# Samples' index scores started inside the second pass of the projections, without a barrier; admission of three prompt tiles set into the prompt attention

## The chip, the cores and the metric

The kernel runs on one core of a Trainium2 chip. The metric is the device time of one execution in microseconds (us), lower is better. The engines are named PE (matrix multiply; PEld is its weight load), DVE (vector), ACT (scalar, activations), POOL (GpSimd) and SP (which here only starts transfers).

## The reference

One step of a hybrid decoder layer over 1024 prompt tokens and 64 sample tokens (8 samples of 8 tokens, each with 2048 past tokens in a paged cache):

```python
u, q, k, v, qi, ki, wi = project(rms_norm(h), w_in)      # one projection, 1864 columns
q, k, qi, ki = rope(...)                                  # partial rotary
pool_o = pool_mix(u_ext, ...)                             # windows 2/4/8/16, then a 128x128 map per group
# indexer: 8 heads, one shared key per token
s = einsum('bthd,bsd->bths', qi, ki) * IDX_DIM ** -0.5
score = einsum('bths,bth->bts', relu(s), wi)              # causal
_, sel = top_k(score, 256)                                # each query keeps 256 keys
attn_o = sparse_attend(q, k[sel], v[sel])                 # prompt: own keys; samples: paged cache and own keys
h = h + concat(pool_o, attn_o) @ w_out
h = h + hier_moe(rms_norm(h), ...)                        # top-2 of 8 experts in 1 of 4 groups
```

## The kernel before

Tokens are cut in nine tiles: eight of 128 prompt tokens and one of the 64 sample tokens, which is worked on first (`ORDER`). The engines run hand-written instruction streams that meet at semaphores, and at four barriers on which all engines wait. PSUM has eight banks; each stage gives them names (`PART` for stage 1, `P2A` for 2a), an order of uses written out by hand (`order`, `orderA`), and a pair of semaphores per bank: PE "claims" a bank (waits until the use before was emptied), another engine "takes" it when it is filled. `SAME` says which bank of stage 2a carries on the counts of which bank of stage 1.

- **Stage 1, first pass.** Keys, values, index queries of each tile; for prompt tiles 2 to 7 the index scores (PE L1079, relu on ACT L1592, weighted sum on DVE L1966). The steps of tile n's scores are a generator, `scores(n)`, of which other loops pull a piece after each of their matmuls.
- **Stage 1, second pass.** For each of nine rounds n: `pool_inputs(n)` (PE L1107), `q_turn(n-1)` (transposes of rotated queries, L1127), `queries(n)` (L1118), `pool_out(n-1)` (L1139), `u_turn(n-1)` (L1150). The last prompt tile's scores are pulled from `pool_inputs(0)`; round 3 begins with the transposes of the pooling state (L1171). POOL computes the windows (`pooling(n)`) and rotates the queries (`rope_q(n)`, L821 to L824). ACT empties the banks (L1533) and between them runs 18 coarse bisection rounds for the prompt tiles 2, 3, 4 ("near"; L1657, L1661, L1665).
- **Beside it, on DVE:** the bisection of each row's threshold. `halve` counts the scores above a middle value (L2002, one pass over the row) and makes three short steps; 26 rounds for the prompt tiles 5, 6, 7 ("far"), then `admit` for each (five long operations, L2026 to L2040, which write the mask), then 10 fine rounds and `admit` for the near tiles, then `masks_ready`.
- **Barrier `phase1`** (PE, ACT, DVE, POOL; SP's loads of `w_out` and the router wait on it too).
- **Stage 2a**, the samples' index scores: for each sample b POOL gathers its 2048 paged index keys (`index_keys(b)`, L895, 512 KB) into one of two buffers, PE turns them (`ki_turn`, L1197), ACT copies them, PE multiplies (`s_scores`, L1208), ACT takes the relu (L1734), and PE sums the heads into three banks with a weight matrix `WD` (`weighted`, L1221) that POOL builds after the barrier (L923, L928). At the end ACT copies the sums into `SCs`, in order of tokens (five copies).
- **Barrier `phase2a`.**
- **Stage 2b**, attention of the prompt tiles: 32 steps (tile i, head pair h). "S": PE multiplies queries and keys (L1249), DVE adds the mask and takes the maximum (L2337), ACT takes the exponential (L1780). "T": PE turns the probabilities (L1260), ACT copies. "V": times the values (L1272). Among them are the output projection (OP, L1302; DVE adds the residual, L2287) and the router's logits. The bisection over the samples' rows (64 x 2056) is done meanwhile on DVE, as a generator `selections()`: after a step of kind S or V of tile i, DVE pulls `PIECES[i][kind]` pieces. Its pieces are: one that does nothing, two reductions (L1977, L1979), 26 rounds of four pieces of which one is a pass (L2002), and the admission.
- **Stage 2c** is the samples' attention, then follow the experts and the last norm.

A second use of memory matters: the two key buffers are `rl` and the last 1024 words; the region behind `w_out`'s place overlays the normalised input `xnT`.

Of the kernel before, what the change touches and what calls it, by code (L numbers as in the profile page):

```python
# [22 lines left out]
P = 128  # L23
# [34 lines left out]
PIECES = [{"S": 2}] + [{"S": 4}] * (NT - 2) + [{"S": 1, "V": 1}]  # L58
# [67 lines left out]
def program(nc, x_prompt, x_sample, cache_k, cache_v, cache_idx_k, state_pool, page_table, norm_mix_g, w_in,  # L126
# [5 lines left out]
    with ctx:  # L132
# [58 lines left out]
        Z = cut(2 * 12 * HD, (2, 12, HD))  # L191
        Zq = cut(2 * NH * HD, (2, NH, HD))
        rt1 = cut(11 * ROPE, (11, ROPE))
        rt2 = cut(11 * ROPE, (11, ROPE))
        rounds = cut(3 * COARSE, (3, COARSE))
# [5 lines left out]
        kin = [v.rearrange("p (s d) -> p s d", s=SLOTS) for v in (rl[:, :, :].rearrange("p a b -> p (a b)"), mem[:, TOTAL - 1024:TOTAL])]  # L201
# [28 lines left out]
        region = at[0]  # L230
        kiTs = cut(2 * 1024, (2, 8, P))
        rs = cut(2 * HLS, (2, HLS))
        zslots = cut(NBLK * 16, None, I32)
        WD = cut(SB * (P + ST))
        assert at[0] <= TOTAL
# [307 lines left out]
        SAME = {"2aACC": "1B4", "2aTR0": "1T0", "2aTR1": "1T1", "2aPS0": "1S0", "2aPS1": "1S1", "2aPS2": "1B5"}  # L543
# [49 lines left out]
        ki_in = [sem(f"ki_in{s}") for s in range(2)]  # L593
# [12 lines left out]
        masks_ready = sem("prompt_masks_ready")  # L606
# [190 lines left out]
        def _(pool):  # L797
# [93 lines left out]
            def index_keys(b):  # L891

                if b >= 2:
                    take(pool, "2a", "TR1", b - 2)
                pool.indirect_dma_start(kin[b % 2].rearrange("p s d -> p (s d)"), None, ci_rows,  # L895
                                        bass.IndirectOffsetOnAxis(ap=pidx[:, b:b + 1], axis=0)).then_inc(ki_in[b % 2], 16)
# [7 lines left out]
            for n in range(TILES):  # L904
                pooling(n)
                rope_q(n)
                if n == 3:
# [7 lines left out]
            copied(pool, "1", "T0", ("q", 0))  # L915
            for g in range(NKV):
                q0 = qT[HD * g:HD * (g + 1), :, SEQ:NTOK].rearrange("p h (b t) -> p b h t", b=SB)
                link(pool.tensor_copy(QB[HD * g:HD * (g + 1), :, g, :, :], q0))
# [3 lines left out]
            pool.wait_ge(phase1, 4)  # L922
# [8 lines left out]
            for b in range(2, SB):  # L931
                index_keys(b)

# [6 lines left out]
            for s in range(2):  # L940
                pool.wait_ge(ki_in[s], 16 * SB // 2)
# [81 lines left out]
        def _(pe):  # L1023
# [73 lines left out]
            def pool_inputs(n, between):  # L1097
# [13 lines left out]
            def queries(n):  # L1111
# [7 lines left out]
                ins.then_inc(filled["1B4"], 1)  # L1119
# [36 lines left out]
            for n in range(TILES):  # L1156
# [5 lines left out]
                for _ in between:  # L1162
                    pass
            between = scores(TILES - 1)
            next(between)
            for n in range(TILES + 1):
                if n == 3:
                    pe.wait_ge(state_in, 16)
                    claim(pe, "1", "T0", "state")
                    for g in range(4):  # L1170
                        ins = tr(ps[:, 0, g * SB * HALO:(g + 1) * SB * HALO], stt_in[0:SB * HALO, g * P:(g + 1) * P], ident(SB * HALO))  # L1171
                    ins.then_inc(filled["1T0"], 1)
                if n < TILES:
                    pool_inputs(n, between)
                    for _ in between:
                        pass
                if n:
                    q_turn(n - 1)
                if n < TILES:
                    queries(n)  # L1180
# [4 lines left out]
            settle(pe, "1")  # L1185
            pe.drain().then_inc(phase1, 1)
            pe.wait_ge(phase1, 4)

            def ki_turn(b):
                pe.wait_ge(ki_in[b % 2], 16 * (b // 2 + 1))
                for c in range(2):
                    claim(pe, "2a", f"TR{c}", b)
                    for j in range(4):
                        a = 2 * (4 * c + j)
                        ins = tr(ps[:, 3 + c, j * P:(j + 1) * P], kin[b % 2][:, a:a + 2, :].rearrange("p s d -> p (s d)"), ident(P))  # L1197
# [31 lines left out]
            for b in range(SB):  # L1229
# [3 lines left out]
                if b:  # L1233
                    weighted(b - 1)
# [294 lines left out]
        def _(act):  # L1529
# [164 lines left out]
            for n in range(TILES + 1):  # L1694
                if n == 3:
                    take(act, "1", "T0", "state")
                    copy(uS[:, :, :, 0:HALO], ps[:, 0, 0:4 * SB * HALO].rearrange("p (g b t) -> p g b t", g=4, b=SB))\
                        .then_inc(emptied["1T0"], 1)
                if n < TILES:
                    keep_u(n)  # L1700
                    some_rounds(n)
# [3 lines left out]
                if n < TILES:  # L1705
                    keep_queries(n)
# [818 lines left out]
```

## Time and profile before

| | us |
|---|---|
| three runs | 1226.13, 1226.91, 1229.39 (median 1226.91) |
| the profiled execution | 1225.94, of which the span of the trace is 1224.10 |
| stage 1 until the barrier | 0 to 334.2 |
| stage 2a until the barrier | 334.2 to 386.6 |
| stage 2b, from the first mask on DVE to the first of tile 7 | 387.65 to 590.96 |
| granted TensorE clock, mean | 0.944 |

In the rows further down a group of instructions stands with its start and its time on the chip; a source line in brackets or behind an arrow is what ended the idle time before it. Windows give the busy time of each engine within a stretch.

### The profile page before, as it was taken

Reading aid. Unit: us, or ns where it says so; the run is one execution under the profiler, and the core shown is the slowest. Engines: PE = TensorE matmul, PEld = TensorE weight load, DVE = VectorE, ACT = ScalarE, POOL = GpSimd, SP = SyncE. Lnnn points to the kernel's source line nnn. Section 1 sums busy time; section 2 is a strip of 40 time slices with the busy share of each in tenths; the row PEclk is TensorE's granted clock in tenths of the full one; section 3 lists DMA queues with packets and bytes.
Section 4 is the critical chain, followed back from the end, with each engine's and each line's share of the span. In section 5 each row is a group of like instructions: output and inputs, shape, how many; then the busy total and the mean of one; then the engine's idle time right before and its main releaser. Section 6 shows DMA issues by size and latency. Waiting matters only on the chain.

```text
span 1224.1 us, 16550 instructions
## 1 busy us (share of the span) xinstructions
PE 1085.3 (89%) x6208; PEld 732.9 (60%) x6208; DVE 581.1 (47%) x1282; ACT 413.1 (34%) x976; POOL 205.7 (17%) x256
## 2 busy tenths in 40 slices
PE   4999989899886999999997898499999999999920
PEld 2554433354343677777775556287878778788720
DVE  2234568999997777666462361213111111111138
ACT  1234445567534345555541333211111110111113
POOL 1432215354421000000012200000000000000032
PEclk9999999999988699999999899699999999999965
DMA  6510000010095911110012741499899999998757
GB/s 215 197 46 12 12 22 1 1 35 5 9 239 198 278 53 52 52 53 35 36 35 78 301 181 70 146 371 372 303 345 339 334 350 329 331 352 326 271 181 281
DMA packets 71372, 209.54 MB, mean 171 GB/s; under 512 B 11214, under 2 KB 31774, under 8 KB 61061
## 3 DMA queue, kind: packets, MB, share of 16 engines
q1 hardware_dynamic: 57119, 151.75, 35.1%
q0 software_dynamic: 10448, 44.21, 10.7%
q10 hardware_dynamic: 3742, 12.75, 2.7%
q8 instruction: 38, 0.62, 0.2%
q14 instruction: 25, 0.20, 0.1%
HBM read 171.40 MB, written 37.40 MB: 171 GB/s over the span
## 4 chain that ended last, share of the span: by engine, by line
PE 80%; DVE 9%; ACT 3%; DMA 3%; issue 2%; POOL 1%; SPq 0%; POOLq 0%; ACTq 0%; DVEq 0%; PEldq 0%
PE ps L1457 18%; PE ps L1463 10%; PE ps L1302 8%; PE ps L1091 5%; PE ps L1107 5%; PE ps L1118 5%; PE ps L1046 3%; PE ps L1079 3%; PE ps L1249 3%; PE ps L1260 2%; PE ps L1450 2%; PE ps L1272 2%; ACT mem L1533 2%; DVE mem L2002 2%; PE ps L1313 1%
## 5 line engine op out<-in xcount | busy, mean ns | idle before, releaser
L1533 ACT ACTIVATE mem<-ps 128x512 f32<-128x512 f32 (+10 forms) x376 | 172.6, 497 | 330.7 <-PE ps L1463 64.1
L1457 PEld LDWEIGHTS ps<-mem 128*128 128x128 f32 x2048 | 235.4, 193 | 16.8 <-issue 16.8
L1457 PE MATMUL ps<-mem 128*128 128x96 f32 x2048 | 234.9, 276 | 0.8 <-DVE mem L2404 0.8
L2002 DVE TENSOR_SCALAR_CACHE_REDUCE mem<-mem 128x768 bf16<-128x768 f32 (+2 forms) x134 | 166.5, 1283 | 0.0
L1302 PE MATMUL ps<-mem 128*128 128x256 f32 (+1 forms) x544 | 126.6, 385 | 5.8 <-ACT mem L1533 2.8
L1463 PE MATMUL ps<-mem 128*96 128x512 f32 x256 | 119.3, 609 | 2.4 <-DVE mem L2396 2.3
L1302 PEld LDWEIGHTS ps<-mem 128*128 128x128 f32 (+1 forms) x544 | 100.1, 189 | 23.1 <-ACT mem L1533 3.7
L2396 DVE TENSOR_TENSOR mem<-mem,ps 128x192 f32<-128x192 f32 x32 | 11.4, 356 | 212.7 <-ACT mem L1873 212.7
L1873 ACT ACTIVATE mem<-ps 128x192 f32<-128x192 f32 x32 | 10.6, 333 | 264.0 <-PE ps L1457 264.0
L983 POOL DMA_INDIRECT mem<-xn_rows,mem x32 | 29.0, 905 | 369.4 <-PE ps L1450 317.6
L1463 PEld LDWEIGHTS ps<-mem 128*96 128x96 f32 x256 | 39.6, 164 | 58.5 <-issue 52.4
L1091 PE MATMUL ps<-mem 128*128 128x512 f32 (+1 forms) x144 | 70.9, 610 | 0.0
L2337 DVE CUSTOM_DVE_ANT_0 mem<-ps,mem 128x128 f32<-128x128 f32 (+7 forms) x64 | 48.2, 754 | 47.0 <-PE ps L1249 47.0
L2411 DVE COPY mem<-ps 96x512 f32<-96x512 f32 x32 | 22.1, 689 | 102.0 <-PE ps L1463 102.0
L1107 PE MATMUL ps<-mem 128*128 128x512 f32 (+1 forms) x192 | 68.1, 505 | 0.0
L1118 PE MATMUL ps<-mem 128*128 128x512 f32 (+1 forms) x144 | 63.4, 593 | 0.0
L1966 DVE SCALAR_TENSOR_TENSOR mem<-mem 128x512 f32<-128x512 f32 (+3 forms) x70 | 47.0, 672 | 19.1 <-ACT mem L1592 14.6
L1260 PE MATMUL ps<-mem 128*128 128x128 f32 x288 | 46.7, 290 | 7.1 <-ACT mem L1780 5.5
L1592 ACT ACTIVATE mem<-ps 128x512 f32<-128x512 f32 (+3 forms) x80 | 38.5, 523 | 38.0 <-PE ps L1079 33.0
L1780 ACT ACTIVATE mem<-mem 128x128 f32<-128x128 f32 (+7 forms) x64 | 49.3, 773 | 5.2 <-DVE mem L2340 5.0
L1107 PEld LDWEIGHTS ps<-mem 128*128 128x128 f32 x192 | 31.3, 194 | 32.9 <-issue 32.9
L1260 PEld LDWEIGHTS ps<-mem 128*128 128x128 f32 x288 | 32.5, 145 | 25.8 <-issue 18.1
(292 smaller groups left out, 1387.2 us busy)
## 6 DMA issues: line engine op xcount, KB each, us to landing
mem<-in_expert_w_gate SPq DMA_DIRECT2D x32, 1024.0 KB, 5.5
mem<-in_expert_w_up SPq DMA_DIRECT2D x32, 1024.0 KB, 8.7
mem<-in_expert_w_down SPq DMA_DIRECT2D x32, 1024.0 KB, 10.9
expert_rows<-mem ACTq DMA_DIRECT2D x32, 384.0 KB, 8.0
expert_rows<-mem SPq DMA_DIRECT2D x2, 4608.0 KB, 30.3
mem<-in_x_prompt SPq DMA_DIRECT2D x16, 512.0 KB, 4.3
mem<-in_w_in SPq DMA_DIRECT2D x3, 2048.0 KB, 10.8
h_rows<-mem SPq DMA_DIRECT2D x8, 512.0 KB, 2.6
```

The source lines that it names most:

```text
L1091: ins = mm(ps[0:r, 4, :], xnT[:, k, tok], w1[:, k, NKI:NIN - CK], start=(k == 0), stop=(k == KC - 1))
L1107: ins = mm(out, w2[:, k, g * P:(g + 1) * P], xnT[:, k, tok], start=(k == 0), stop=(k == KC - 1))
L1118: ins = mm(ps[0:r, 4, :], xnT[:, k, tok], w2[:, k, CQ:CK], start=(k == 0), stop=(k == KC - 1))
L1260: ins = tr(ps[:, 4 + part, (j - c) * P:(j - c + 1) * P], Sm[:, u % 2, g, j * P:(j + 1) * P], ident(P))
L1302: ins = mm(ps[0:r, 7, 0:256], lhs, wout[:, k, 256 * t[2]:256 * t[2] + 256], start=(k == 0), stop=(k == last))
L1457: ins = mm(ps[:, 2 + s, j * CAP:(j + 1) * CAP], wgu[w][:, j // 2, k, (j % 2) * P:(j % 2 + 1) * P], xgT[:, s, k, :], start=(k == 0), stop=( ...
L1463: ins = mm(ps[0:CAP, 5 + c, :], hT[:, s, k, :], wdn[w][:, k, 512 * c:512 * (c + 1)], start=(k == 0), stop=(k == 1))
L1533: return fn(out, in_, ACT.Copy, scale=scale)
L1780: fn(probs, probs, ACT.Exp, bias=nb[:, c:c + 1], scale=SCALE, accum_out=esum[:, 8 * (i % 2) + c:8 * (i % 2) + c + 1]).then_inc(s_exp, 1)
L1966: v.scalar_tensor_tensor(out=dst, in0=src, scalar=wt, in1=dst, op0=ALU.mult, op1=ALU.add).then_inc(score_added, 1)
L2002: v.tensor_scalar(bufs[a % 3][0:R, 0:w], sc, mid[:, a:a + 1], None, ALU.is_ge, ALU.add, accum_out=cnt[:, a:a + 1]).then_inc(step, 1)
L2337: v.tensor_tensor_reduce(out=Sm[:, u % 2, g, 0:w], in0=sc2, in1=maskv(i), scale=1.0, scalar=-3e38, op0=ALU.add, op1=ALU.max, accum_out=mx[ ...
```

## The change

Seven edits, all in the order of work and in the place of buffers; the arithmetic is the same.

1. Four key buffers in place of two. Buffers 2 and 3, the turned keys `kiTs` and the relus `rs` lie over `xnT`, `WD` over the rotated queries `Zq`. POOL issues the gathers 2 and 3 right behind its last `rope_q`, waits for all four, and builds `WD` as soon as the last queries were turned, before the barrier.
2. PE goes from round 8 of the second pass straight on to stage 2a: `ki_turn(0)`, `s_scores(0)`, `ki_turn(1)`, then the last queries, pooling and state turns, then samples 1 to 7. The barrier `phase1` is signalled by PE after `ki_turn(2)`, by ACT after `keep_ki(3)`; neither waits on it. SP and POOL still do.
3. The bank names of 2a are laid on other counts of stage 1.
4. In the second pass the last prompt tile's scores are pulled from the fourth matmul of `pool_inputs(0)` on and from `queries(0)`; before, their first step (the transposes of `z_turn(8)`) stood ahead of `pool_inputs(0)`.
5. The turn of the pooling state moves from the start of round 3 to behind `queries(3)`.
6. The last copy of 2a is shared: ACT copies the even slots, DVE the odd ones; ACT runs a small exponential ahead of it.
7. DVE's admission of the near tiles moves behind the barrier `phase2a`, into the generator of stage 2b, ahead of the samples' selection (18 pieces and the first of `select`, the nineteenth). `PIECES` grows from 112 to 136 in all. The first gathers of stage 2c, which wait on `masks_ready`, move with it; the clearing of the overflow rows no longer waits on it.

```diff
-PIECES = [{"S": 2}] + [{"S": 4}] * (NT - 2) + [{"S": 1, "V": 1}]
+PIECES = [{"S": 2, "V": 1}, {"S": 1, "V": 1}] + [{"S": 5, "V": 1}] * 2 + [{"S": 4, "V": 1}] * 3 + [{"S": 1, "V": 1}]
...
-            if n == 3:
-                order += [("T0", "state")]
...
+                if n == 3:
+                    order += [("T0", "state")]
...
-        SAME = {"2aACC": "1B4", "2aTR0": "1T0", "2aTR1": "1T1", "2aPS0": "1S0", "2aPS1": "1S1", "2aPS2": "1B5"}
+        SAME = {"2aACC": "1T0", "2aTR0": "1S3", "2aTR1": "1B4", "2aPS0": "1B5", "2aPS1": "1S0", "2aPS2": "1S1"}
...
-                if b >= 2:
-                    take(pool, "2a", "TR1", b - 2)
+                if b >= 4:
+                    take(pool, "2a", "TR1", b - 4)
...
-            for s in range(2):
+            for b in (2, 3):
+                index_keys(b)
+            for s in range(4):
                 pool.wait_ge(ki_in[s], 16)
...
             pool.wait_ge(kv_out, 48 * TILES)
             pool.drain().then_inc(phase1, 1)
-            pool.wait_ge(phase1, 4)
+            take(pool, "1", "T0", ("q", TILES - 1))
             link(pool.memset(WD[:, :], 0.0))
...
-            for b in range(2, SB):
+            for b in range(4, SB):
                 index_keys(b)
+            pool.wait_ge(phase1, 4)
...
+            pool.wait_ge(phase2a, 3)
+            pool.memset(zrow, 0.0).then_inc(zrow_ready, 1)
             pool.wait_ge(masks_ready, 1)
             past(Kin, ck_rows, 0, K_in)
             past(Kin, ck_rows, 1, K_in)
-            pool.wait_ge(phase2a, 3)
             past(Vin, cv_rows, 0, V_in)
-            pool.memset(zrow, 0.0).then_inc(zrow_ready, 1)
...
-                        next(between, None)
+                        if k >= 3:
+                            next(between, None)
...
             between = scores(TILES - 1)
-            next(between)
-            for n in range(TILES + 1):
...
+            for n in range(TILES):
+                pool_inputs(n, between)
                 if n:
                     q_turn(n - 1)
-                if n < TILES:
-                    queries(n)
+                queries(n, between)
+                for _ in between:
+                    pass
+                if n == 3:
+                    state_turn()
                 if n:
                     pool_out(n - 1)
...
-            settle(pe, "1")
-            pe.drain().then_inc(phase1, 1)
-            pe.wait_ge(phase1, 4)
...
             ki_turn(0)
-            for b in range(SB):
+            s_scores(0)
+            ki_turn(1)
+            q_turn(TILES - 1)
+            pool_out(TILES - 1)
+            u_turn(TILES - 1)
+            for b in range(1, SB):
                 s_scores(b)
                 if b + 1 < SB:
                     ki_turn(b + 1)
-                if b:
-                    weighted(b - 1)
+                if b == 1:
+                    settle(pe, "1")
+                    pe.drain().then_inc(phase1, 1)
+                weighted(b - 1)
...
+            fn(stat[:, 254:255], const("z"), ACT.Exp)
             take(act, "2a", "ACC", 0)
...
-            for a in range(2):
-                for q in range(2):
-                    copy(inorder[:, 8 * q + a:8 * q + a + 7:2, :], ps[a * SR:(a + 1) * SR, q, :].rearrange("r (s p) -> r s p", s=4))
+            for q in range(2):
+                copy(inorder[:, 8 * q:8 * q + 7:2, :], ps[0:SR, q, :].rearrange("r (s p) -> r s p", s=4))
...
+            act.wait_ge(odd_slots_kept, 1)
...
             halvings(near, 0, FINE)
-            admit_group(near, 0)
-            dve.nop().then_inc(masks_ready, 1)
+            take(dve, "2a", "ACC", 0)
+            inorder = SCs[0:SR, 0:PAST].rearrange("r (p s) -> r s p", s=SLOTS)
+            for q in range(2):
+                ins = v.tensor_copy(inorder[:, 8 * q + 1:8 * q + 8:2, :], ps[SR:2 * SR, q, :].rearrange("r (s p) -> r s p", s=4))
+            ins.then_inc(odd_slots_kept, 1)
...
             def selections():
+                unhalve(near, 0)
+                for a, entry in enumerate(near):
+                    yield from admit(entry, a)
+                dve.nop().then_inc(masks_ready, 1)
+                near_admitted.append(True)
                 yield from select([(SCs[0:SR, :], LS, SR, const("tailmask", SR), None, (sJ, sG, sT))], 6, sample_step, admitted)
```

## Rows read from the trace of the kernel before

**Rows 1.** The page's busy times and share of the span, instructions.

```profile
PE 1085.3 (89%) x6208; PEld 732.9 (60%) x6208; DVE 581.1 (47%) x1282; ACT 413.1 (34%) x976; POOL 205.7 (17%) x256
```

**Rows 2.** Stretch, length, busy PE, PEld, DVE, ACT, POOL, granted clock, DMA share, GB/s.

```profile
192.94:336.65 143.71, 133.60 (x396) 64.25 (x395) 139.20 (x298) 85.69 (x268) 71.23 (x92) 0.97 0.04 11
336.65:365.20 28.55, 22.77 (x88) 13.56 (x87) 27.03 (x103) 10.77 (x24) 4.92 (x6) 0.84 0.97 255
365.20:380.00 14.80, 14.80 (x58) 8.31 (x57) 13.83 (x26) 6.75 (x15) 2.71 (x5) 1.00 0.18 60
380.00:387.65 7.65, 3.30 (x13) 1.71 (x12) 0.38 (x5) 3.92 (x5) 2.70 (x3) 0.93 0.74 265
```

**Rows 3.** PE in order of time where the second pass begins.

```profile
171.29 0.99 PE L1061 MATMUL ps<-mem 128*128 128x128 f32 x4 [3.30 <-POOL mem L836]
174.34 1.38 PE L1079 MATMUL ps<-mem 64*128 64x512 f32 x4
190.45 7.08 PE L1118 MATMUL ps<-mem 128*64 128x512 f32 x16
```

**Rows 4.** The chain of waits around round 3 and at the end of the second pass.

```profile
227.10 0.02 issue
...
232.87 8.57 PE ps L1107 x16
...
317.90 6.88 PE ps L1118 x16
```

**Rows 5.** POOL in order of time: first queries rotated, last ones, `WD`.

```profile
201.67 0.45 POOL L824 TENSOR_TENSOR mem<-mem 64x128 f32<-64x128 f32 x1
...
280.41 0.32 POOL L822 TENSOR_TENSOR mem<-mem 128x64 f32<-128x64 f32 x1
...
326.12 1.05 POOL L822 TENSOR_TENSOR mem<-mem 128x64 f32<-128x64 f32 x1
...
334.25 1.01 POOL L923 MEMSET mem<- 128x1088 f32 x1 [4.58 <-ACTq L1718]
335.34 1.43 POOL L928 TENSOR_TENSOR mem<-mem 64x64 f32<-64x64 f32 x2
```

**Rows 6.** The gathers of index keys: all eight, then the two of round 3.

```profile
DMA to landing us min/median/max: 4.1/6.7/10.9
...
mem<-in_cache_idx_k,mem POOLq DMA_INDIRECT x2, 4.4
```

**Rows 7.** PE in stage 2a: the wait for keys, the sums at either clock.

```profile
348.08 1.97 PE L1197 MATMUL ps<-mem 128*128 128x128 f32 x8 [5.53 <-DMA mem<-in_cache_idx_k,mem]
349.84 3.27 PE L1221 MATMUL ps<-mem 128*128 128x512 f32 x6
355.81 2.01 PE L1221 MATMUL ps<-mem 128*128 128x512 f32 x6
```

**Rows 8.** Copies at 2a's end on ACT, table load, DVE's nearest copies from PSUM.

```profile
382.63 3.94 ACT L1533 ACTIVATE mem<-ps 64x512 f32<-64x512 f32 x5 [3.43 <-PEq L1226]
388.22 1.28 ACT L1780 ACT_TABLE_LOAD   x1 [1.65 <-DVE mem L2340]
...
411.49 0.68 DVE L2277 TENSOR_TENSOR mem<-ps,mem 128x512 f32<-128x512 f32 x1
```

**Rows 9.** Busy time in tiles 0, 1, 2, 3 and 4 to 6 of stage 2b.

```profile
387.65:403.01 15.36, 8.65 (x36) 4.46 (x36) 13.10 (x38) 6.53 (x24) 0.39 (x2) 0.50 1.02 323
403.01:425.67 22.66, 21.07 (x96) 13.88 (x96) 17.19 (x55) 7.79 (x25) 0.00 (x0) 0.69 1.01 294
425.67:451.86 26.19, 25.82 (x160) 18.87 (x161) 20.47 (x57) 14.28 (x32) 0.00 (x0) 1.00 0.18 64
451.86:482.56 30.70, 30.18 (x204) 22.79 (x205) 21.74 (x59) 16.06 (x32) 0.00 (x0) 1.00 0.15 52
482.56:590.96 108.40, 106.20 (x790) 82.40 (x791) 71.69 (x174) 59.95 (x119) 0.00 (x0) 1.00 0.12 45
```

**Rows 10.** One pass of the samples' bisection on DVE.

```profile
427.63 2.34 DVE L2002 TENSOR_SCALAR_CACHE_REDUCE mem<-mem 64x2056 bf16<-64x2056 f32 x1
```

More of the change, by code:

```diff
@@ L592, in program @@
         pidx_ready = sem("page_rows_ready")
-        ki_in = [sem(f"ki_in{s}") for s in range(2)]
+        ki_in = [sem(f"ki_in{s}") for s in range(4)]
         sample_step = sem("sample_step")
@@ L906, in _ @@
                 rope_q(n)
+                if n == 2:
+                    copied(pool, "1", "T0", ("q", 0))
+                    for g in range(NKV):
+                        q0 = qT[HD * g:HD * (g + 1), :, SEQ:NTOK].rearrange("p h (b t) -> p b h t", b=SB)
+                        link(pool.tensor_copy(QB[HD * g:HD * (g + 1), :, g, :, :], q0))
                 if n == 3:
@@ L939, in _ @@
             pool.wait_ge(slots_cleared, 16)
-            for s in range(2):
-                pool.wait_ge(ki_in[s], 16 * SB // 2)
+            for s in range(4):
+                pool.wait_ge(ki_in[s], 16 * SB // 4)
             pool.drain().then_inc(phase2a, 1)
@@ L1118, in queries @@
                     ins = mm(ps[0:r, 4, :], xnT[:, k, tok], w2[:, k, CQ:CK], start=(k == 0), stop=(k == KC - 1))
-                ins.then_inc(filled["1B4"], 1)
+                    if k == KC - 1:
+                        ins.then_inc(filled["1B4"], 1)
+                    next(between, None)
             def q_turn(n):
@@ L1163, in _, with state_turn @@
                     pass
-            between = scores(TILES - 1)
-            next(between)
-            for n in range(TILES + 1):
[L1167 to L1172, printed above, removed]
-                if n < TILES:
-                    pool_inputs(n, between)
-                    for _ in between:
-                        pass
+            def state_turn():
+                pe.wait_ge(state_in, 16)
+                claim(pe, "1", "T0", "state")
+                for g in range(4):
+                    ins = tr(ps[:, 0, g * SB * HALO:(g + 1) * SB * HALO], stt_in[0:SB * HALO, g * P:(g + 1) * P], ident(SB * HALO))
+                ins.then_inc(filled["1T0"], 1)
+            between = scores(TILES - 1)
+            for n in range(TILES):
+                pool_inputs(n, between)
                 if n:
                     q_turn(n - 1)
-                if n < TILES:
-                    queries(n)
+                queries(n, between)
[3 more added lines that the diff above has]
+                    state_turn()
                 if n:
@@ L1692, in some_rounds, with keep_state, keep_ki, relus_of @@
                     next(between, None)
[L1694 to L1701, printed above, removed]
+            def keep_state():
+                take(act, "1", "T0", "state")
+                copy(uS[:, :, :, 0:HALO], ps[:, 0, 0:4 * SB * HALO].rearrange("p (g b t) -> p g b t", g=4, b=SB))\
+                    .then_inc(emptied["1T0"], 1)
+            def keep_ki(b):
+                for c in range(2):
+                    take(act, "2a", f"TR{c}", b)
+                    copy(kiTs[:, b % 2, 4 * c:4 * c + 4, :], four(ps[:, 3 + c, :], P)).then_inc(emptied[f"2aTR{c}"], 1)
+            def relus_of(b):
+                for q in range(3):
+                    w = 512 if q < 2 else ST
+                    take(act, "2a", f"PS{q}", b)
+                    if b >= 2 and q == 0:
+                        act.wait_ge(sec_done, b - 1)
+                    fn(rs[:, b % 2, 512 * q:512 * q + w], ps[:, 5 + q, 0:w], ACT.Relu).then_inc(emptied[f"2aPS{q}"], 1)
+            for n in range(TILES):
+                keep_u(n)
+                some_rounds(n)
                 if n:
@@ L1704, in _ @@
                     some_rounds(n)
[L1705 to L1707 removed]
+                keep_queries(n)
+                if n == 3:
+                    keep_state()
+                some_rounds(n)
                 if n:
@@ L1714, in _ @@
                 pass
+            keep_ki(0)
+            relus_of(0)
+            keep_ki(1)
+            keep_q(TILES - 1)
+            keep_pool(TILES - 1)
+            keep_u_turned(TILES - 1)
             copied(act, "1", "T0", ("u", TILES - 1))
             act.dma_start(pool_prompt[0, 0], ut[0:HALO, :]).then_inc(u_out, 16)
[L1717 to L1734 removed]
+            for b in range(1, SB):
+                relus_of(b)
                 if b + 1 < SB:
                     keep_ki(b + 1)
+                if b == 2:
+                    act.wait_ge(u_out, 16 * (SB + 1))
+                    act.drain().then_inc(phase1, 1)
+            fn(stat[:, 254:255], const("z"), ACT.Exp)
             take(act, "2a", "ACC", 0)
             inorder = SCs[0:SR, 0:PAST].rearrange("r (p s) -> r s p", s=SLOTS)
[L1739 to L1742 removed]
+            for q in range(2):
+                copy(inorder[:, 8 * q:8 * q + 7:2, :], ps[0:SR, q, :].rearrange("r (s p) -> r s p", s=4))
+            copy(SCs[0:SR, PAST:LS], ps[0:SR, 2, 0:ST])
+            act.wait_ge(odd_slots_kept, 1)
+            act.nop().then_inc(emptied["2aACC"], 1)
             act.drain().then_inc(phase2a, 1)
```

45 lines of the change are left out of this document (16 added, 29 removed).

## The prediction

> **What bounds the kernel now.** The page comes first: PE is busy 89% of the span, DVE 47% [rows 1]. As averages these point at PE and hide the stretch that matters. The view by stretches shows it: from 192.94 to 336.65 DVE is busy 139.20 of 143.71 us (bounds, 26 rounds, admission of the far tiles), to 365.20 it is busy 27.03 of 28.55 us (the fine rounds of the near tiles), to 380.00 it is busy 13.83 of 14.80 us (their admission); then it stands for 7 us [rows 2]. PE in the same stretches is busy too, but with a second pass and stage 2a whose end nobody but stage 2b needs. So two chains run side by side to the start of 2b: DVE's, without holes until 380.00, and PE's, with holes. PE's comes last, at 386.6 [rows 8]. Whatever shortens PE's chain gains only down to DVE's, and DVE's needs its own cut; the change makes both.
>
> The PE views in order of time give PE's holes: 3.30 us for the rotation of the last keys at 171.29, with a slow start behind it [rows 3]; 227.10 to 232.87 at round 3, with 0.6 us of work of its own, and 8.57 us for the sixteen matmuls behind it where 6.9 is the rule [rows 4]; from 324.8 to 334.25 the tail of the second pass and the barrier [rows 4, 5]; 5.53 us for the third gather [rows 7].
>
> **PE's chain after the change.**
> - Start of the second pass. Three matmul pairs of `pool_inputs(0)` (3 x 0.86 = 2.6 us; sixteen matmuls take 6.88 [rows 4]) now fill the 3.30 us. Without the slow start the first scores come about 1.3 us before 174.34, and so do all DVE times from 192.94 on. PE has four of the eight k-steps of `queries(0)` behind it when the scores end (3.5 us). Together 4.8 us. But the next queries turn needs POOL's rotation, which ended at 202.1 [rows 5] and starts only 1.3 us earlier: PE is held about 1.2 us. Gain 3.6.
> - Round 3. The hole is there because the state turn's bank waits for ACT's copy behind five bisection pieces. Behind `queries(3)` that copy is long done. 5.77 - 0.6 = 5.2 less, and 1.7 for the slow matmuls behind it; `pool_out(1)` and the turn behind it, some 1.1 us, lie in the hole and stay. Gain 5.8. So the second pass ends at 324.8 - 9.4 = 315.4.
> - Stage 2a. POOL's last rotation ends 4.0 us later (324.8 to 328.85 before), 319.4. Gathers 2 and 3 are issued by 321.6 and land by 326 at 4.4 us each [rows 6]. `WD` costs 1.01 + 1.43 plus gaps, 2.7 us, behind their landing: 328.8. PE meanwhile does `ki_turn(0)` to `s_scores(1)`, `ki_turn(2)` and the last turns (316.3 to 326.2), then stands 2.6 us for `WD`. Before, from the start of the first sums at 349.84 to the end at 382.5 it was 32.7 us, at a cold first group (3.27 where 2.01 is the rule [rows 7]): 31.4 warm. PE's sums are ready at 328.8 + 31.4 = 360.2. Gathers 4 to 6 are issued by 332, ahead of SP's loads, which wait for the barrier (ACT behind `keep_ki(3)`, about 334); gather 7 has over 10 us.
> - SP's loads of `w_out` thus start when they did before (334.2) and are first needed in tile 1 of 2b: no cost. SP's queue holds nothing else. The clearing of 9.2 MB starts some 20 us sooner and ahead of the K gathers; nobody waits for either until 2c.
>
> **DVE's chain after the change.** 365.20 - 1.3 = 363.9, later than PE's 360.2, so DVE decides. Its two copies of 64 x 512 from PSUM aren't in the trace. Below: 0.68 each, its own 128 x 512 operation; above: 0.95, ACT's strided ones (3.94 for four and a small one) [rows 8]. I take 0.8, since the store is strided: 365.5; two more semaphores, 365.8 for the first matmul of 2b against 386.67. ACT's half ends by 362.2 and is hidden. **Start of 2b: -20.9 us** (bounds -21.5 and -18: if the gathers land in 10.9 us like the one in the worst row [rows 6], `WD` comes at 335 and PE's chain ends at 367; ACT and DVE add 2).
>
> **Stage 2b.** Now the 14.80 us of admission must be done before the masks of tile 2. Count the pieces: tiles 0 and 1 pulled 24 of the samples' selection, now 19, of which 18 are admission. In DVE's time: 24 pieces are two reductions of 2.3 and 5.2 rounds of 2.9 (a pass of 2.34 [rows 10] and four short steps), some 20 us; 19 are 14.8. From step to step:
> - Tile 0 took 15.36 us with DVE 13.10 busy and PE at half clock [rows 9]. The table load of 1.28 us [rows 8] is done ahead; the pieces of the small tiles are short. I get steps of 2.4, 3.2, 2.6 and 3.7: 11.9. Tile 1 is bound by PE at half clock (21.07 busy of 22.66): about 21.4. Gain 4.7.
> - Tiles 2 and 3 pull 24 pieces each, not 16: two rounds, 5.8 us more per tile. Tile 2 has 26.19 - 20.47 = 5.7 us of DVE idle, tile 3 has 9.0 [rows 9]: the sum fits, but not evenly. Five pieces at S hold one pass or two, and S(2,0) gets both reductions and a pass (6.9 us). DVE's residual adds queue behind them, and PE's next claim of bank 7 behind those. Against the old gaps between masks S(2,0) is 4.5 late, S(2,1) 1.8, S(3,1) 2.1: 8.4 if nothing hides it, 3.3 if PE's work between its scores and its turns (about 3 us) hides its part. I take 5.5.
> - Tiles 4 to 6 pull one piece more at each V, a whole pass in one V per tile. DVE is idle 36.7 of 108.4 us there. I take 1 us, bounds 0 and 3.
> - Tile 7 has fewer pieces left than before: 0.
>
> Net for 2b: -4.7 + 5.5 + 1 = **+1.8**, bounds -5 and +7. Stages 2c, experts and last norm are as before; the K gathers land some 290 us before 2c.
>
> [...] POOL's step L822 took 0.32 us while DVE counted and 1.05 while it admitted tiles with two inputs from SBUF [rows 5]. [...]
>
> The table load is 1.28 us in its row [rows 8]; "ScalarE: Activation LUTs", section "What ACT_TABLE_LOAD costs", of the Trainium skill gives 2.66 with its drain. By the one tile 0 gains 1.3, by the other 2.7; no row here shows the drain.
>
> **The sum.** Against the profiled execution of 1225.94: -20.9 + 1.8 = -19.1, 1206.8. The three runs' median stands 1.0 higher. I say **1207**.
>
> **The rivals.**
> - *A, as above: DVE's fine rounds set the start of 2b, 2b about even.* 1202 to 1213. Chance 0.66.
> - *B, 2b becomes DVE's.* All 14.8 us of the admission come back as time, since DVE was busy 13.10 of 15.36 in tile 0 and 20.47 of 26.19 in tile 2. Against: PE was busy 21.07 of 22.66 in tile 1, and five pieces less are pulled ahead of tile 2. 1225.9 - 20.9 + 14.8 = 1220. Chance 0.12.
> - *C, PE's chain decides after all:* slow gathers, the port, `WD` late, a half clock behind the 2.6 us wait. 1225.9 - 18 + 1.8 = 1210, and with a stall at each of gathers 4 to 6 (5.5 each) up to 1218. For: 10.9 us in one row. Against: PE has 3.7 us of slack, and four gathers are landed or under way. Chance 0.07.
> - *D, the double passes are hidden.* In before PE hardly waits for DVE in tiles 2 and 3 (25.82 of 26.19, 30.18 of 30.70 busy). 1225.9 - 20.9 - 4.7 = 1200, less if tile 1 leaves half clock sooner. Chance 0.12.
> - *E, slower.* Every step of tiles 2 and 3 exposes a whole round: PE claims bank 7 for the next projection, the claim waits for the residual add, and that stands behind the five pieces. 8 x 2.9 = 23.2, so 1228 to 1231. It decides only from 20.9 / 2.9 = 7.2 exposed rounds on; the two tiles get four rounds more in all, and their DVE idle of 14.7 us speaks against it. Chance 0.03.
>
> **Range and chances.** 1207 from A. The range 1199 to 1215 takes in A, D and most of C, leaving out B and E. About 0.3% of the time, 4 us, is what a measurement can tell from nothing. Faster by more: A, B (6 us), C, D: 0.94; within: 0.03, a B or C gone worse; slower: 0.03.
>
> **What would show it.** Right: DVE goes from its last fine round into the two copies with hardly a wait, about 364, and PE's sums are ready some 4 us before; first mask of 2b near 366.8; the turn of the state without a wait; PE's second pass ending near 315.4; tile 2's first mask near 400, tile 4's near 463. Wrong: DVE waiting for the sums at its copies (C); masks of tiles 2 and 3 each late with no idle time on DVE (B, E); tile 1 at full clock from its start (D, and lower).

## The result: 1217.9 us, and the profile after

The changed kernel takes 1217.9 us (median of 4 runs, 1216.23 to 1218.22); the kernel before, beside it, 1227.09 (4 runs, 1226.13 to 1229.39). The ratio is 0.992, interval 0.9903 to 0.9937: faster by 9 us, where 20 were forecast. The profiled execution took 1218.01 us, its span is 1216.2, against 1225.94 and 1224.10: 7.9 us less. The working below is made on these two.

The page says nothing of this, as before [rows 1]: nearly the same instructions and busy shares.

```profile
PE 1079.9 (89%) x6208; PEld 732.2 (60%) x6208; DVE 580.9 (48%) x1284; ACT 411.7 (34%) x975; POOL 205.8 (17%) x256
```

The view by stretches of the kernel after, with the columns of [rows 2]: the first three lines reach to the first mask of stage 2b, then come tiles 0, 1, 2, 3 and 4 to 6, each from its first mask to the next tile's.

```profile
190.90:333.85 142.95, 134.37 (x420) 66.56 (x419) 138.21 (x300) 91.09 (x282) 74.28 (x95) 0.99 0.05 16
333.85:362.40 28.55, 28.55 (x113) 16.37 (x112) 27.04 (x103) 12.63 (x28) 4.95 (x7) 0.96 0.93 238
362.40:368.85 6.45, 3.91 (x16) 1.94 (x14) 2.25 (x8) 3.48 (x7) 0.21 (x1) 1.00 0.24 86
368.85:380.25 11.40, 8.43 (x36) 4.22 (x36) 10.37 (x41) 5.72 (x24) 0.00 (x0) 0.57 1.01 309
380.25:400.77 20.52, 19.34 (x95) 13.02 (x96) 12.20 (x40) 7.28 (x24) 0.77 (x1) 0.74 1.00 291
400.77:437.24 36.47, 28.60 (x160) 20.17 (x161) 30.41 (x74) 14.57 (x32) 2.12 (x3) 0.93 0.44 160
437.24:474.27 37.03, 32.25 (x204) 24.53 (x205) 27.20 (x70) 15.99 (x32) 0.00 (x0) 0.93 0.12 43
474.27:583.98 109.71, 106.46 (x791) 82.54 (x792) 79.15 (x193) 60.57 (x119) 0.00 (x0) 1.00 0.12 44
```

Set against [rows 9], this is the ledger: the first mask comes at 368.85 instead of 387.65 (-18.8); tiles 0 and 1 take 31.9 instead of 38.0 (-6.1); tiles 2 and 3 take 73.5 instead of 56.9 (**+16.6**); tiles 4 to 6 take 109.7 instead of 108.4 (+1.3). Sum -7.0, and 0.9 comes behind it. So 25 us were won ahead of tile 2 and 17 given back in two tiles. In those two the granted clock fell to 0.93, from 1.00 before.

The chain of waits of the kernel after (start, length, what), at round 3, at the end of the second pass, and from there to the first sums of stage 2a:

```profile
200.90 0.46 POOL mem L830
201.41 0.46 PE ps L1140 x4
...
239.11 0.41 PE ps L1181 x4
...
308.69 6.88 PE ps L1129 x16
...
320.72 5.18 DMA mem<-in_cache_idx_k,mem
326.10 2.60 POOLq L929
328.69 0.11 issue
328.80 1.02 POOL mem L932
329.89 0.99 POOL mem L937
330.95 1.32 POOL mem L937
332.32 4.01 PE ps L1229 x6
```

PE is held for POOL's rotation at 200.90, as forecast; the turn of the state (L1181) follows its neighbours without a hole; the second pass ends at 315.58 (forecast 315.4). Then a term appears that the forecast hadn't: 2.60 us on POOL's queue at L929, its drain for the barrier, which stands ahead of `WD`. The chain of waits of the kernel before had such a row too, for the same drain (L920 there), ahead of the barrier:

```profile
329.71 2.44 POOLq L920
```

What follows `WD` in the kernel after, in the views in order of time of PE, ACT and DVE:

```profile
332.32 4.01 PE L1229 MATMUL ps<-mem 128*128 128x512 f32 x6 [6.97 <-POOL mem L937]
...
362.53 1.28 ACT L1759 ACT_TABLE_LOAD   x1
...
365.94 1.88 ACT L1548 ACTIVATE mem<-ps 64x512 f32<-64x512 f32 x3 [1.92 <-PEq L1234]
```

```profile
366.01 1.87 DVE L2161 COPY mem<-ps 64x512 f32<-64x512 f32 x2 [3.62 <-PEq L1234]
```

DVE was done with its fine rounds at 362.4 and waited 3.62 us for the sums. The forecast had it the other way round: sums ready at 360.2, DVE at 363.9. The sums were ready at 365.8, 5.6 us later than said: 3.5 because they began at 332.32 and not at 328.8, and 2.1 because they took 33.5 us for 31.4. The forecast had taken full clock, but behind PE's wait of 6.97 us the first group took 4.01 us for 2.01, and the granted clock from 332.30 to 339.10 is 0.70; from 339.10 on it is 1.00. The copies cost 1.87 (1.6 said), and the table load lies in the wait.

### Where tiles 2 and 3 lose their time

First the kernel before, DVE in the first step of tile 2. Behind the pass at 427.63 [rows 10] comes the residual add (L2287), and then DVE waits for PE's next scores:

```profile
429.90 0.41 DVE L2287 TENSOR_TENSOR mem<-ps,mem 128x256 f32<-128x256 f32 x1
...
431.40 0.56 DVE L2337 CUSTOM_DVE_ANT_0 mem<-ps,mem 128x384 f32<-128x384 f32 x1 [0.52 <-PE ps L1249]
```

Of the 14.7 us that DVE is idle in tiles 2 and 3, 11.4 are such waits, one in each of the eight steps.

DVE in order of time at the start of tile 2 (kernel after):

```profile
402.10 2.28 DVE L2001 TENSOR_REDUCE mem<-mem 64x1 f32<-64x2056 f32 x1
404.30 2.28 DVE L2003 TENSOR_REDUCE mem<-mem 64x1 f32<-64x2056 f32 x1
...
407.30 2.33 DVE L2026 TENSOR_SCALAR_CACHE_REDUCE mem<-mem 64x2056 bf16<-64x2056 f32 x1
...
409.94 0.43 DVE L2314 TENSOR_TENSOR mem<-ps,mem 128x256 f32<-128x256 f32 x1
```

and PE in the same place:

```profile
400.92 3.62 PE L1317 MATMUL ps<-mem 128*128 128x256 f32 x16
410.43 5.41 PE L1317 MATMUL ps<-mem 128*128 128x256 f32 x16 [3.49 <-DVE mem L2314]
...
418.06 0.66 PE L1301 MATMUL ps<-mem 128*128 128x128 f32 x4 [1.42 <-DVE mem L2314]
```

PE's waits between 400 and 475, summed by what they waited for (total, times, longest):

```profile
PE ps L1322 <- DVE mem L2314: 5.0, 2, 2.6
PE ps L1301 <- DVE mem L2314: 3.8, 2, 2.4
PE ps L1317 <- DVE mem L2314: 3.5, 1, 3.5
```

The projection of 400.92 was finished at 404.5, but its residual add (L2314) stands behind three long operations and runs at 409.94. PE's next projection waits for it, 3.49 us, and then takes 5.41 us for what takes 3.62 elsewhere: after the wait PE is at a lower granted clock (0.68 from 410.43 to 415.80, where it was 1.00 from 400.77 to 410.93; from 404.5 to 410.4 PE had been busy 2.4 of 5.9 us). In the kernel before, PE's waits for the residual add make 0.3 us between 387 and 484; here the three rows make 12.3. Step by step, first mask to first mask, before and after: (2,0) 5.7 and 10.2, (2,1) 6.6 and 9.0, (2,2) 6.1 and 6.2, (2,3) 7.8 and 11.1; (3,0) 8.5 and 9.0, (3,1) 7.2 and 9.6, (3,2) 6.7 and 6.7, (3,3) 8.3 and 11.7. The five long ones are (2,0), which has both reductions and a pass ahead of its add, and (2,1), (2,3), (3,1), (3,3), which have two passes ahead of it. DVE's idle time stayed as it was, 6.1 and 9.8 us in the two tiles for 5.7 and 9.0 before: none of the extra work went into it.

### The profile page after: what moved, and what is told of

It reads as the page before. It is cut to its first block, busy times and chain, and to the rows that moved or that the text cites. A ratio compares the mean times of both kernels' runs of the same rounds, so it can differ in the third digit from the quotient of the medians.

```text
span 1216.2 us, 16556 instructions
## 1 busy us (share of the span) xinstructions
PE 1079.9 (89%) x6208; PEld 732.2 (60%) x6208; DVE 580.9 (48%) x1284; ACT 411.7 (34%) x975; POOL 205.8 (17%) x256
## 4 chain that ended last, share of the span: by engine, by line
PE 76%; DVE 13%; DMA 3%; issue 2%; ACT 2%; POOL 2%; SPq 0%; POOLq 0%; ACTq 0%; DVEq 0%; PEldq 0%
PE ps L1472 18%; PE ps L1478 10%; PE ps L1317 6%; PE ps L1101 5%; PE ps L1129 5%; PE ps L1117 5%; DVE mem L2026 4%; PE ps L1056 4%; PE ps L1089 3%; PE ps L1264 2%; PE ps L1465 2%; PE ps L1275 2%; DVE mem L2372 2%; PE ps L1287 2%; PE ps L1328 1%
## 5 line engine op out<-in xcount | busy, mean ns | idle before, releaser
L1548 ACT ACTIVATE mem<-ps 128x512 f32<-128x512 f32 (+9 forms) x374 | 170.5, 495 | 317.0 <-PE ps L1275 62.9
L2431 DVE TENSOR_TENSOR mem<-mem,ps 128x192 f32<-128x192 f32 x32 | 11.4, 356 | 213.5 <-ACT mem L1897 213.5
L1101 PE MATMUL ps<-mem 128*128 128x512 f32 (+1 forms) x144 | 70.9, 610 | 0.0
L1117 PE MATMUL ps<-mem 128*128 128x512 f32 (+1 forms) x192 | 64.7, 489 | 0.0
L1129 PE MATMUL ps<-mem 128*128 128x512 f32 (+1 forms) x144 | 64.3, 595 | 0.0
L1990 DVE SCALAR_TENSOR_TENSOR mem<-mem 128x512 f32<-128x512 f32 (+3 forms) x70 | 47.0, 672 | 19.0 <-ACT mem L1607 14.4
L1275 PEld LDWEIGHTS ps<-mem 128*128 128x128 f32 x288 | 33.1, 147 | 23.0 <-issue 18.8
```

The costliest lines, as they stand in the source:

```text
L1101: ins = mm(ps[0:r, 4, :], xnT[:, k, tok], w1[:, k, NKI:NIN - CK], start=(k == 0), stop=(k == KC - 1))
L1129: ins = mm(ps[0:r, 4, :], xnT[:, k, tok], w2[:, k, CQ:CK], start=(k == 0), stop=(k == KC - 1))
L1275: ins = tr(ps[:, 4 + part, (j - c) * P:(j - c + 1) * P], Sm[:, u % 2, g, j * P:(j + 1) * P], ident(P))
L1548: return fn(out, in_, ACT.Copy, scale=scale)
```

## The experiments

Nine, in three batches. Each ratio is to the kernel before on the same chip.

**1. The same number of pieces, spread level.** Tiles 2 and 3 give one piece less per step, the last tile takes them.

```diff
-... + [{"S": 5, "V": 1}] * 2 + [{"S": 4, "V": 1}] * 3 + [{"S": 1, "V": 1}]
+... + [{"S": 4, "V": 1}] * 5 + [{"S": 2, "V": 1}]
```

> Theory L (lumps): in tiles 2 and 3 of stage 2b time is lost only in the steps whose five pieces hold two long operations ahead of the residual add that frees bank 7. With 4 pieces at every S of tiles 2 to 6, each S holds one pass; the four double steps (+2.4, +3.3, +2.5, +3.4 us in the changed kernel's trace) go back to the old length, S(2,0) stays long, and about two more passes at a V cost 0.5 to 0.8 each: 1218 - 10 = 1208. Theory T (load): DVE simply has too much to do in the two tiles; what counts is its total. Then only the eight pieces taken out (two rounds, 5.8 us) come off, and come back in part in later tiles: 1212 to 1215.

Measured 1222.58 (1218.74 to 1224.99, 9 runs), ratio 0.9968 (0.9952 to 0.9984): slower than the change, both expectations missed. Yet tiles 2 and 3 took 67.4 us in place of 73.5, and the last mask of 2b came at 606.96 in place of 613.78. The 6.8 us, and 2.4 more in the profiled executions, are lost behind it, where the samples' selection now ends too late. DVE and POOL at the end of 2b, in order of time:

```profile
609.62 4.42 DVE L2055 TENSOR_TENSOR_SCAN mem<-mem 64x2056 f32<-64x2056 bf16 x1
...
625.71 4.67 DVE L2384 COPY mem<-mem 128x512 f32<-128x512 f32 x1
```

```profile
620.75 9.34 POOL L968 TENSOR_SCALAR mem<-mem 64x2048 bf16<-64x2048 bf16 x1
```

The scan stands in the last steps, and the copy of 0.43 us lasts 4.67 and ends just behind POOL's operation of 9.34. By PE's waits the scan costs more than the copy: scan and pass stand ahead of a residual add (616.65), for which PE waits 3.96 us at 617.14, with a granted clock of 0.83 over the ten us behind it (1.00 in the same place of the changed kernel). The projection behind the copy waits 1.60 us in place of 0.29.

**2. The same pieces in the same steps, one of them behind the residual add.** This is the run that parts the theories: in tiles 2 and 3 four pieces at S, the fifth once the residual add is issued.

```diff
-... + [{"S": 5, "V": 1}] * 2 + [{"S": 4, "V": 1}] * 3 + [{"S": 1, "V": 1}]
+... + [{"S": 4, "V": 1}] * 5 + [{"S": 1, "V": 1}]
...
-                if i < NT:
+                if kind == "S":
+                    step_tile = i
+                if kind == "OP" and step_tile in (2, 3):
+                    some_pieces(1)
+                elif i < NT:
                     some_pieces(PIECES[i].get(kind, 0))
```

> The same number of pieces in each tile as in the changed kernel, but in tiles 2 and 3 the fifth piece of a step is pulled behind DVE's residual add, not ahead of it. Theory L: the double steps shorten, since PE's next claim of bank 7 no longer waits behind a second pass: 1218 - 8 to - 11 = 1207 to 1210. Theory T: DVE's load per tile is unchanged, so the time is too: 1217 to 1219.

Measured 1209.02 (1207.99 to 1210.28, 4 runs), ratio 0.9859 (0.9843 to 0.9874): 8 to 9 us better than the change (8.9 by the medians, 7.5 by the two ratios), with the pieces of every tile unaltered. Tiles 2 and 3 took 64.0 us in place of 73.5. So 9.5 of the 16.6 us are the order within a step, not the load. What is left against the 56.9 of before sits where a step holds more than one long operation: (2,0), with both reductions and a pass ahead of the add, stays at 10.05 against 5.73. A second pass behind the add costs 1.8 us in (2,1) and 0.8 in (3,1), and nothing in (2,3) and (3,3), which last 7.8 and 8.3 us as before the change.

**3. Only the admission put back** ahead of the last copies, where it stood before, with the pieces of before; all else as changed.

```diff
             halvings(near, 0, FINE)
+            admit_group(near, 0)
+            dve.nop().then_inc(masks_ready, 1)
...
             def selections():
-                unhalve(near, 0)
-                for a, entry in enumerate(near):
-                    yield from admit(entry, a)
-                dve.nop().then_inc(masks_ready, 1)
```

> Everything of the change but edit 7: the near tiles are admitted ahead of the last copy of 2a and PIECES is the old list. If DVE's chain then decides the start of 2b, its fine rounds end at 362.3, admission at 377, copies at 379, first mask at about 380.5 against 368.85; stage 2b is then as before less the table load. 1227 - 7 - 1.3 = about 1218.5, the same as the changed kernel: the move of the admission won 11.7 us ahead of 2b and lost it in tiles 2 and 3. If it were PE's chain that decides throughout, the time would be no later than the changed kernel's start of 2b with the old tiles: 1227 - 18.8 - 1.3 = 1207.

Measured 1216.54 (1215.67 to 1218.28, 4 runs), ratio 0.9926 (0.9911 to 0.9942). Here DVE is the later chain; windows of this kernel from the start of its fine rounds to their end and on to the first mask:

```profile
333.00:362.40 29.40, 29.40 (x117) 16.72 (x117) 27.95 (x106) 14.23 (x30) 4.59 (x6) 0.98 0.91 234
362.40:378.59 16.19, 2.38 (x10) 1.26 (x8) 14.72 (x28) 1.89 (x3) 0.83 (x2) 0.68 0.07 29
```

The first mask comes at 378.59, 9.7 us later than with the change. Up to the first mask of tile 2 the changed kernel is 14.4 us ahead of this one (400.77 and 415.12), since tiles 0 and 1 are shorter too. Tiles 2 and 3 take 56.9 us here and 73.5 there, 4 to 6 108.4 and 109.7. So edit 7 wins 9.7 us ahead of 2b and 4.6 in tiles 0 and 1 and, as it is placed, loses 17.9 in tiles 2 to 6. The ratios (0.9926 and 0.992) don't tell the two kernels apart.

**4. POOL's drain behind `WD`.** POOL still waits for all four gathers; its drain for the barrier moves from ahead of `WD` to behind it, and with it the wait for `kv_out`, which takes 0.04 us in the chain (326.01).

```diff
-            pool.wait_ge(kv_out, 48 * TILES)
-            pool.drain().then_inc(phase1, 1)
             take(pool, "1", "T0", ("q", TILES - 1))
             link(pool.memset(WD[:, :], 0.0))
...
                 pool.wait_ge(weights_spread, a + 1)
+            pool.wait_ge(kv_out, 48 * TILES)
+            pool.drain().then_inc(phase1, 1)
```

> POOL's drain ahead of the barrier (2.6 us in the trace) stands behind the building of WD, not ahead of it. If PE's chain decides the start of 2b in the changed kernel (sums ready at 365.8, DVE's fine rounds done at 362.3), the sums are ready 2.6 us earlier and the time falls by 2.5 us, to 1215.4. If DVE's chain decides, as the prediction had it, nothing changes.

Measured 1215.87 (1214.8 to 1218.34, 5 runs), ratio 0.9921 (0.9907 to 0.9935): 2.0 us under the change's median, but its ratio to the kernel before is that of the change (0.992), so the runs show no certain gain in time. The trace shows the mechanism: the sums begin 3.7 us sooner, and the first mask comes at 365.49, 3.4 us sooner, while DVE's fine rounds end where they did. PE's chain sets the start of 2b in the changed kernel. PE, then DVE, in order of time:

```profile
328.66 2.63 PE L1228 MATMUL ps<-mem 128*128 128x512 f32 x6 [3.33 <-POOL mem L934]
```

```profile
362.41 1.92 DVE L2160 COPY mem<-ps 64x512 f32<-64x512 f32 x2
```

DVE goes from its fine rounds into the copies without a wait, at 362.41. That is the state that the forecast had taken for the changed kernel's.

**5. Both, 2 and 4.**

> The two edits of x2_behind_add (fifth piece behind the residual add) and x4b_drain_behind (POOL's drain behind WD) together on the changed kernel. They act in different stretches, so they should add: 1217.9 - 8.9 - 2.0 = 1207. If the one only moves a wait into the other's stretch, it stays at 1209.

Measured 1207.44 (1206.02 to 1209.83, 5 runs), ratio 0.984 (0.982 to 0.9861). Against experiment 2 nothing certain is gained (1209.02 and 1207.44, the intervals of the ratios overlap); in its profiled execution the first mask came at 368.98. The last section tells why.

**6. The two reductions moved to tile 1**, so that no step of tile 2 has three long operations.

```diff
-PIECES = [{"S": 2, "V": 1}, {"S": 1, "V": 1}] + ...
+PIECES = [{"S": 2, "V": 1}, {"S": 2, "V": 1}] + ...
...
-                if kind == "OP" and step_tile in (2, 3):
+                if kind == "OP" and step_tile == 3:
```

> As y1_both, but tile 1 pulls two pieces at S (not one), and tile 2 none behind the residual add; the total of 136 stays. Both long reductions and the first pass then fall in tile 1, where DVE is busy 12.2 of 20.5 us, and S(2,0) holds one pass. Theory L: S(2,0) falls from 10.0 to about 6 and S(2,1) from 8.4 to 6.6, tile 1 grows by 0 to 2: 1207 - 4 to - 6 = 1201 to 1203. Theory T (load of DVE): the three long operations cost the same wherever they stand: 1206 to 1208.

Measured 1207.38 (1206.08 to 1211.67, 5 runs), ratio 0.9845 (0.9822 to 0.9869): a miss, nothing gained on experiment 5. Step (2,0) fell to 5.75 us, but (2,2) stands at 8.3 and (2,3) at 9.2, where a pass now falls on a V of tile 2, and tile 1 paid 2.9 us in its four steps (against 18.98 in experiment 5; against the 20.24 of experiment 2, with the same pieces in tile 1, it is 1.6). What a second pass behind the add costs hangs on the step: 2.2 us in (2,2) here, nothing in (3,3). Why is not shown.

**7. Level as in 1, but the selection finished sooner** by a second piece at V in tiles 5 and 6.

```diff
-... + [{"S": 4, "V": 1}] * 5 + [{"S": 2, "V": 1}]
+... + [{"S": 4, "V": 1}] * 3 + [{"S": 4, "V": 2}] * 2 + [{"S": 1, "V": 1}]
```

> x1_level won 6.8 us by tile 7's last mask against the changed kernel and lost more than that behind it: its samples' selection ended late, POOL's mask operation (9.3 us) fell on DVE's copy of the inverse sums, which took 4.67 us in place of 0.43, and its scan stood ahead of the last projections' adds. Here the same level pieces in tiles 2 and 3, but tiles 5 and 6 pull two pieces at V, so that the selection ends eight pieces sooner. If that collision is the cause: the copy is back at 0.43 and the time 1209 to 1213. If the level pieces themselves are bad: 1219 to 1222 as before.

Measured 1213.66 (1212.93 to 1214.13, 4 runs), ratio 0.9888 (0.9867 to 0.991). POOL's long operation now runs from 600.91, and the copy at 623.60 takes 0.43 us again. So the late selection was what cost experiment 1 its gain. The time is 0.7 us above the 1213 expected, and POOL's operation still holds DVE up: it now falls on DVE's multiplication of 1.29 us (L2323), which lasts 4.87 from 605.85, as it does in the changed kernel (4.38).

**8. The edits of the second pass undone** (4 and 5): the transposes ahead of `pool_inputs(0)`, the state turn at the start of round 3.

```diff
-                        if k >= 3:
-                            next(between, None)
+                        next(between, None)
...
-                    next(between, None)
...
             between = scores(TILES - 1)
+            next(between)
             for n in range(TILES):
+                if n == 3:
+                    state_turn()
                 pool_inputs(n, between)
+                for _ in between:
+                    pass
```

> The changed kernel with edits 4 and 5 undone: the state turn at the start of round 3 and the last prompt tile's scores pulled as before. PE's second pass should end 9.2 us later (324.8 for 315.6). PE's chain decides the start of 2b by 3.6 us already, so all of it comes through: 1227. Were DVE's chain the one that decides, only what goes beyond it: 9.2 less the slack that PE's chain has, 3 to 6 us, 1221 to 1224.

Measured 1228.01 (1227.5 to 1232.51, 10 runs), ratio 1.0009 (0.9997 to 1.0022): no gain over the kernel before. PE and DVE of this kernel in order of time:

```profile
341.92 4.01 PE L1228 MATMUL ps<-mem 128*128 128x512 f32 x6 [6.18 <-POOL mem L937]
```

```profile
376.06 1.94 DVE L2160 COPY mem<-ps 64x512 f32<-64x512 f32 x2 [9.64 <-PEq L1233]
```

The sums begin 9.6 us later than with the change (341.92 for 332.32), and DVE waits 9.64 us for them instead of 3.62; the first mask comes at 378.96, 10.1 later. The forecast of -9.4 for these two edits is borne out, and the median moves by the same ten.

**9. At most one pass ahead of a residual add, and none extra in tiles 2 and 3.** Experiment 5 with the extra pieces in tile 1 and in tiles 4 to 6, whose steps are longer; there they stand behind the residual add.

```diff
-PIECES = [{"S": 2, "V": 1}, {"S": 1, "V": 1}] + [{"S": 4, "V": 1}] * 5 + [{"S": 1, "V": 1}]
+PIECES = [{"S": 2, "V": 1}, {"S": 2, "V": 1}] + [{"S": 4}] * 2 + [{"S": 4, "V": 1}] * 3 + [{"S": 1, "V": 1}]
...
-                if kind == "OP" and step_tile in (2, 3):
+                if kind == "OP" and step_tile in (4, 5, 6):
```

> y3_reductions_in_tile1 brought nothing against y1_both: what it took from S(2,0) came back as a pass at a V of tile 2 (+2.2 us there, against 0.5 to 0.8 in tiles 4 to 6). So in tiles 2 and 3 one round per step is all that fits. Here tiles 2 and 3 pull four pieces at S and none else (as before the change), tile 1 two at S, and tiles 4 to 6 take the rest: four at S, one behind the residual add, one at V. If it is so, tiles 2 and 3 return to 57 us (from 64), tiles 4 to 6 grow by 2 to 3: 1207.4 - 4 to - 5 = 1202 to 1204. If any long operation costs about its own length wherever it stands: 1206 to 1208.

Measured 1201.21 (1199.41 to 1203.03, 5 runs), ratio 0.9799 (0.9779 to 0.9819): better than both kernels, 24 us under the one before. Windows of tiles 2, 3 and 4 to 6:

```profile
402.37:428.58 26.21, 25.76 (x158) 18.80 (x159) 20.57 (x60) 13.89 (x31) 0.00 (x0) 1.00 0.53 185
428.58:459.30 30.72, 30.19 (x204) 22.79 (x205) 21.77 (x58) 16.06 (x32) 0.00 (x0) 1.00 0.14 52
459.30:567.88 108.58, 106.30 (x791) 82.50 (x792) 87.26 (x209) 59.94 (x119) 0.00 (x0) 1.00 0.13 45
```

Tiles 2 and 3 take 56.9 us as before the change [rows 9], and the clock stays at 1.00. Tiles 4 to 6 took over the extra DVE work, 87.3 us busy in place of 71.7, for 0.2 us. Tile 1 pays 1.4 us against the change.

## Why the prediction was wrong, point by point

- **The second pass, -9.4.** Right: it ends at 315.58 for 315.4, with the hold for the rotation at 200.90 and the turn of the state without a hole; experiment 8 gives it back.
- **Stage 2a, `WD` at 328.8.** Wrong by 3.5 us. The gathers landed as said (325.9), but POOL's drain for the barrier, 2.60 us, stands ahead of `WD`, and I had costed the wait and not the drain; the multiplication (L937) took 2.38 for 1.43. The drain had a row of its own in the trace before, 2.44 us, inside the stretch that I read as "the tail of the second pass and the barrier". The trace of experiment 4 shows that this part is on the path.
- **"DVE decides".** Wrong for that reason: DVE was earlier than said (362.4 for 363.9), the sums later (365.8 for 360.2), by `WD` and by the lower clock behind PE's wait. It is the place of rival C: of its causes `WD` late and the half clock came, and the port as the 0.95 us that the multiplication took longer beside DVE's two-input operations (last section); the gathers were not slow. It cost 2 us of the forecast: -18.8 for -20.9, within the bounds given.
- **Tiles 0 and 1, -4.7.** Measured -6.1; tile 0 came as worked out (11.4 for 11.9), tile 1 at 20.5 for 21.4, its clock at 0.74 for 0.69. Of the two prices of the table load the rows bear out the smaller: ACT's last relu ends at 362.51, the load runs from 362.53 to 363.81, and the next activation starts at 363.82.
- **Tiles 2 and 3, +5.5: the step that failed.** Measured +16.6, outside the 8.4 that I gave for "if nothing hides it". I had set the idle time that DVE has in these tiles (5.7 and 9.0 us) against the extra work, and called the others than (2,0), (2,1) and (3,1) free, (2,3) and (3,3) among them. But that idle time lies behind the residual add, where DVE waits for PE's next work. The three steps that I did price came at 4.4, 2.4 and 2.5 us, 9.3 for my 8.4, and nothing hid any of it. Long operations ahead of the add delay DVE's add, then PE's claim, then PE's projection, at a lower clock as well, and then DVE's next input; (2,3) and (3,3) paid 3.3 and 3.4 us, a whole round and more each. Rival E had this mechanism, bank 7's claim behind five pieces. I gave it 0.03, since the sum of idle time spoke against it, and since by its own sum it needed all eight steps to turn the sign. (That sum, 1228, left out the 4.7 us of tiles 0 and 1; with them eight exposed rounds make some 1224, still no slower kernel.) Five paid about a round or more, and that halved the gain without turning it. Experiment 2 shows that the order makes 9.5 us of it, 2 and 6 together that the rest lies in steps with more than one long operation, though not in every such step, and 9 that with one it costs nothing.
- **Rivals B and C.** B's 1220 and C's upper end of 1218 lie near the measured time by luck. C's needed stalls at gathers 4 to 6, and PE was busy for all of 339.10 to 365.80. B had DVE's load come back as time, but tiles 0 and 1, which hold the admission, got shorter, and with the same pieces experiment 2 is 9.5 us shorter in tiles 2 and 3. The sign that I gave for B and E, late masks with no idle time on DVE, was wrong as well: the masks came late and the idle time stayed.
- **Tiles 4 to 6, +1.** Measured +1.3.
- **The range.** Its upper end took in C and left E out whole, so E's mechanism at a part of its price had no place in it. Five exposed rounds of 2.9 us make 14.5 in place of 5.5, and the forecast 1216. (The sum itself gives 1206.8 and 1.0, so 1208; I wrote 1207.)

**To carry to other kernels.** Idle time summed over a stretch is no room for work; ask between which two links of the loop between the engines it lies, and put filler behind the operation that the other engine waits for, and measure where it still costs. When work moves into a filler stream, count the long operations per step and not the pieces, and look at what the stream's end releases. A drain ahead of a barrier is a term of the sum like any other when something on the path is queued behind it.

## What the runs showed of the hardware

**POOL waits for DVE's two-input operations.** The same two multiplications of `WD` (64 x 64) took 0.68 us in experiment 8, where DVE beside them counted (L2025, one input), 1.43 before, 2.38 with the change and 3.47 in experiment 9. In the last case DVE ran two two-input operations back to back, then POOL was done 0.1 us behind their end:

```profile
327.25 1.27 DVE L2052 SCALAR_TENSOR_TENSOR mem<-mem 128x1024 bf16<-128x1024 f32 x1
328.56 2.29 DVE L2054 TENSOR_TENSOR_SCAN mem<-mem 128x1024 f32<-128x1024 bf16 x1
```

```profile
327.48 3.47 POOL L934 TENSOR_TENSOR mem<-mem 64x64 f32<-64x64 f32 x2
```

In experiment 4, with the same code up to here, POOL began 0.4 us sooner, took 1.53 us and was done at 328.61, as the scan began (328.49); PE's sums began at 328.66 there and at 331.00 in experiment 9. In the four profiled executions with the drain behind `WD` the multiplications took 1.53, 3.55, 3.57 and 3.47 us, in five of the six with it ahead 2.25 to 2.48 (the change, experiments 1, 2, 3 and 7; the sixth is experiment 8 with its 0.68): so the 2.60 us of the drain were worth some 1.5 in three of the four (2.60 less 1.1), and the 3.7 of experiment 4 is a lucky case. It explains in part why experiment 5's first mask comes no sooner than experiment 2's (368.98 and 368.99): its sums begin 1.3 us sooner (331.21 and 332.52). The rest is PE's clock: in the first groups, 331.20 to 339.00, it is 0.62, in experiment 2 from 332.50 to 339.20 it is 0.72, and the second group of sums begins only 0.2 us sooner (338.93 and 339.16). That the two-input form is what holds POOL is read off these times; no run changed DVE's operation alone.

**And DVE waits for POOL.** In experiment 1 a copy of 128 x 512 that takes 0.43 us elsewhere lasted 4.67, from 625.71 to 630.38, while POOL's operation ran from 620.75 to 630.09. The Trainium skill, "SBUF — State Buffer", section "SBUF: two separate sides", says that GpSimd and DVE share a port pair, which a DVE operation takes in its two-port modes, or with two inputs from SBUF against a GpSimd operation that reads SBUF, and that whichever starts first holds it for its whole instruction; these rows agree in both directions. The gathers of samples 2 and 3, issued inside the admission, landed in 4.7 us (median of the two), against 4.4 beside counting [rows 6]: hardly slower.

**A drain on POOL costs 2.6 us** with nothing queued ahead of it but finished gathers (326.10, POOLq L929), the largest single term that the forecast of stage 2a left out. The chains of waits of experiments 1, 2, 7 and 8 show the same 2.60, that of the kernel before 2.44, behind two small copies.
